# S5 stage of a two-layer encoder: C powers shared between GpSimd and VectorE, start reordered, gate joined to the scan

## The reference

```
u = x @ w_in                                   # 1024 x 1024, 64 groups of 16 channels
lam_bar = exp(lam * step);  b_bar = ((lam_bar - 1) / lam) * b
h_t = lam_bar * h_(t-1) + b_bar @ u_t          # complex, 64 states per group, both directions
y = Re(c @ h) forward + backward + d_skip * u
y = gelu(y);  y = y * sigmoid(y @ w_glu + b_glu);  y @ w_out
```

## Time and profile before

| | |
|---|---|
| median of 3 runs | 3157.04 us |
| the profiled execution's own time | 3158.34 us |
| its span | 3156.5 us |
| start of the 8 scans on VectorE | 96.3, 137.3, 180.3, 218.1, 252.9, 290.6, 324.5, 352.0 us |
| last product of the gate | ends at 500.84 us |

### The profile page before, as it was taken

One profiled execution on the slowest core, in us unless ns is written; L12 is line 12 of the kernel. 1 busy time (PEld: TensorE's weight loads), 2 busy tenths in 40 slices (PEclk: granted clock), 3 DMA queues, 4 the chain that ended last, 5 costly groups with the idle time before them and its releaser, 6 DMA issues. The chain is left out here.

```text
span 3156.5 us, 37141 instructions
## 1 busy us (share of the span) xinstructions
PE 2795.4 (89%) x14372; PEld 2350.9 (74%) x14372; DVE 1446.9 (46%) x2328; ACT 591.5 (19%) x843; POOL 764.4 (24%) x524
## 2 busy tenths in 40 slices
PE   5477588879999999968999999999687999999995
PEld 4366466668888888856888888889476888888884
DVE  5757622463332333262556555556646332233326
ACT  2122233021111111122222222221302111111111
POOL 1899423121221112211011111010402112111122
PEclk7788788989999999988999999996798999999997
DMA  3133212121111111012010100000312111111101
GB/s 115 47 93 96 67 54 107 40 80 40 40 53 53 53 40 40 13 67 53 21 34 20 33 27 27 26 20 1 120 41 77 44 40 53 53 48 45 40 13 67
DMA packets 213106, 157.94 MB, mean 50 GB/s; under 512 B 21792, under 2 KB 196000, under 8 KB 211872
## 3 DMA queue, kind: packets, MB, share of 16 engines
q1 hardware_dynamic: 213024, 156.83, 16.5%
HBM read 139.04 MB, written 17.76 MB: 50 GB/s over the span
## 5 line engine op out<-in xcount | busy, mean ns | idle before, releaser
L463 PE MATMUL ps<-aT_hi,ffn_w_hi 128*128 128x512 f32 x1408 | 555.6, 395 | 18.0 <-PEq L233 18.0
L463 PE MATMUL ps<-aT_hi,ffn_w_lo 128*128 128x512 f32 x1408 | 553.2, 393 | 0.0
L463 PE MATMUL ps<-aT_lo,ffn_w_hi 128*128 128x512 f32 x1408 | 548.2, 389 | 0.0
L546 DVE TENSOR_TENSOR ffn_act_out<-ffn_act_out,ps 128x512 f32<-128x512 f32 x88 | 60.5, 687 | 710.9 <-ACT ffn_act_out L518 710.9
L563 DVE TENSOR_TENSOR h<-h,ps 128x512 f32<-128x512 f32 x352 | 241.8, 687 | 214.6 <-PE ps L477 212.4
L611 POOL CAST ffn_hid_hi<-ffn_act_out 128x512 fp32r<-128x512 f32 x88 | 57.5, 653 | 1114.4 <-PE ps L477 584.4
L463 PEld LDWEIGHTS ps<-aT_hi,ffn_w_hi 128*128 128x128 f32 x1408 | 265.4, 189 | 72.3 <-issue 18.7
L463 PEld LDWEIGHTS ps<-aT_hi,ffn_w_lo 128*128 128x128 f32 x1408 | 265.1, 188 | 61.3
L463 PEld LDWEIGHTS ps<-aT_lo,ffn_w_hi 128*128 128x128 f32 x1408 | 265.2, 188 | 59.6
L477 PE MATMUL ps<-ffn_w_hi,ffn_hid_hi 128*128 128x512 f32 x704 | 275.9, 392 | 6.8 <-POOL ffn_hid_lo L614 6.8
L477 PE MATMUL ps<-ffn_w_hi,ffn_hid_lo 128*128 128x512 f32 x704 | 275.1, 391 | 0.0
(11 more groups left out here) (246 smaller groups left out, 4359.9 us busy)
## 6 DMA issues: line engine op xcount, KB each, us to landing
ffn_w_raw<-in_ffn_w_in_dram SPq DMA_DIRECT2D x88, 512.0 KB, 5.1
ffn_w_raw<-in_ffn_w_out_dram SPq DMA_DIRECT2D x22, 1024.0 KB, 5.0
hg_w_raw<-in_hg_w_in_dram SPq DMA_DIRECT2D x40, 512.0 KB, 4.0
h<-in_x_dram SPq DMA_DIRECT2D x4, 1024.0 KB, 9.1
s_w_raw<-in_s_w_in_dram SPq DMA_DIRECT2D x8, 512.0 KB, 5.1
s_scratch_u<-h SPq DMA_DIRECT2D x16, 256.0 KB, 2.3
s_u_grp<-s_scratch_u SPq DMA_DIRECT2D x64, 64.0 KB, 2.5
s_pw_in<-s_scratch_kern SPq DMA_DIRECT2D x64, 64.0 KB, 2.5
```

The costliest lines, as they stand in the source:

```text
L463: ins = t.matmul(ps[:, 2 * b + a, :], w[q][:, a, kk, :], x[:, kk, rows], start=(kk == 0 and m == 0), stop=(kk == KT - 1 and m == 2))
L546: v.tensor_tensor(act_out[u % 2][:, :], act_out[u % 2][:, :], ps[:, 2 * (u % 2) + 1, :], ALU.mult).then_inc(s_prod, 1)
```

## The change

Four edits, all in the first 501 us.

1. C powers. GpSimd makes only the backward half of cl (from block 1 on). The forward half is made by VectorE ahead of each scan (`make_cl_in_psum`): ScalarE copies the block's C into PSUM bank 2 (`place_c`), the temporary lies in bank 3, and every product has one operand in PSUM. b_all and c_all are stored with the 16 channels of a group contiguous.
2. Start. All 16 transposes and splits of x come before `tables_to_factors`. `scan_factors` squares with four instructions per level in place of six, and the mask of the diagonal moves ahead of the split of x. GpSimd makes bl of block 1 before cl of block 0.
3. The loop's order. TensorE starts with two blocks of `turn_bl` and `start_state` ahead of the loop, and a turn is now `start_state(n)`, `make_kern(n)`, `within_chunks(n-1)`, `across_chunks(n-1)`, `inputs(n+2)`, `turn_bl(n+1)`. y goes straight to its row of h and from there to DRAM.
4. Gate. Weights of the gate are loaded, split and multiplied in the same block: the splits of y rows 0 to 6 and the gate's tiles 0 and 1 up to row 6 stand before the last y. The buffers of `w_in` and bl take the gate's weights.

```diff
+    def make_cl_in_psum(e, n):
+        link = Steps(S["cl_fw"], (n - 1) * CLF)
+        for b in range(2):
+            rows_ = slice(2 * b, 2 * b + 2)
+            c = [bc(c_turned[:, q, rows_, :], 2, [P, 2, L + 1, GRP]) for q in range(2)]
+            out = [cl[n % 2][:, q, rows_] for q in range(2)]
+            t = ps[:, 3, 0:2 * (L + 1) * GRP].rearrange("p (r l c) -> p r l c", r=2, l=L + 1)
+            product_steps(link, e, c, powers(n, 0, rows_), out, t, conj=True)
...
             for n in range(KT):
+                if n == 0:
+                    put_u(2)
+                else:
+                    ungroup_y(n - 1)
                 if 1 <= n < KT - 1:
                     regroup_u(n + 1)
-                if n >= 1:
-                    ungroup_y(n - 1)
                 place_toeplitz(n)
...
+                if n == KT - 2:
+                    load_glu(0)
+            load_glu(1)
             ungroup_y(KT - 1)
...
-            for n in range(KT):
+            for n in range(1, KT):
+                if n >= 2:
+                    start_state(n)
                 make_kern(n)
-                if n >= 1:
-                    across_chunks(n - 1)
+                within_chunks(n - 1)
+                across_chunks(n - 1)
                 if n + 2 < KT:
                     inputs(n + 2, (0, 1))
                 if n + 1 < KT:
                     turn_bl(n + 1)
-                within_chunks(n)
-                if n + 1 < KT:
-                    start_state(n + 1)
...
+            gate_part(0, (0, 1), range(6), (2, 3))
+            within_chunks(KT - 1)
             across_chunks(KT - 1)
+            gate_part(0, (0, 1), (6,), (2, 3))
+            t.wait_ge(S["glu_lo1"], 1)
+            gate_part(1, (0, 1), range(7), (4, 5))
+            gate_part(0, (0, 1), (7,), (2, 3))
+            gate_part(1, (0, 1), (7,), (4, 5))
...
+            def place_c(n):
+                a.wait_ge(S["min_kept"], 4 * (n + 1))
+                a.activation(c_turned, c_all[:, 0, :, n * PR:(n + 1) * PR, :], ACT.Copy).then_inc(S["c_placed"], 1)
...
+                if n == KT - 2:
+                    split_glu(0)
                 if n + 1 < KT:
                     place_b(n + 1)
                     keep_min(n + 1)
+                    place_c(n + 1)
+                gelu(n - 1)
...
+                if n >= KT - 2:
+                    for kk in (range(5) if n == KT - 2 else range(5, 7)):
+                        split_y(kk)
+                if n == KT - 1:
+                    split_glu(1)
                 keep_state(n)
```

More of the change, by code:

```diff
@@ L88, in __init__ @@
         self.nc, self.ctx = nc, ctx
-        self.phase = None
+        self.phase, self.areas, self.deferred = None, [], False
         self.fresh, self.old = [], []
@@ L1229, in _ @@
             split_w(2)
-            for n in range(KT):
+            keep_min(1)
+            place_c(1)
+            keep_u(2)
+            split_w(3)
+            keep_state(0)
+            keep_kern_rows(0)
+            place_b(1)
+            for n in range(1, KT):
                 keep_kern_rows(n)
-                if n >= 1:
-                    keep_y(n - 1)
+                keep_y(n - 1)
                 if n + 2 < KT:
@@ L1245, in _ @@
             gelu(KT - 1)
+            split_y(KT - 1)
+            gates(0)
+            for n in range(1, KT):
+                if n + 1 < KT:
+                    split_glu(n + 1)
+                gates(n)
         @block.vector
@@ L1423, in _ @@
             tables_to_angles()
-            for n in range(2):
+            channel_mask()
+            for n in range(XT):
                 split_x(n)
             tables_to_factors()
-            for n in range(2, XT):
-                split_x(n)
             v.wait_ge(S["b_kept"], 4)
@@ L1434, in _ @@
             v.memset(state[:, :, :, 0], 0.0).then_inc(S["pads"], 1)
+            scan(0)
+            for n in range(1, KT):
+                v.wait_ge(S["c_placed"], n)
+                if n >= 2:
+                    v.wait_ge(S["out_done"], n - 1)
+                make_cl_in_psum(v, n)
+                scan(n)
+            v.wait_ge(S["y_hi"], KT)
+            v.tensor_tensor(k.aT_lo[:, KT - 1, :], row(KT - 1), k.aT_hi[:, KT - 1, :].bitcast(F32), ALU.subtract
+                            ).then_inc(S["y_lo_last"], 1)
             for n in range(KT):
-                scan(n)
+                for half in range(2):
+                    v.wait_ge(S["gated"], 2 * n + half + 1)
+                    o = h[:, n, half * HALF:(half + 1) * HALF]
+                    v.tensor_tensor(o, o, gate[half][:, :], ALU.mult).then_inc(S["mixed"], 1)
         @block.gpsimd
@@ L1585 @@
+                    ins(n + 1)
+                if n + 3 < KT:
+                    split_w(n + 3)
+            split_glu(0)
+            for n in range(7):
+                split_y(n)
+                if n == 5:
+                    split_glu(1)
+            for n in range(2, KT):
+                split_glu(n)
+    k.close_area()
 HG_OUTS = 5
```

324 lines of the change are left out of this document (158 added, 166 removed).

## The result

The changed kernel takes 3101.2 us (median of 4 runs, 3100.69 to 3106.75), the kernel before 3158.1 in the same comparison (4 runs, 3156.69 to 3162.84): a ratio of 0.9821, 95% interval 0.9804 to 0.9838, so 1.6 to 2.0% faster. The forecast was 3105 us, in a range of 3080 to 3128. The profiled execution took 3100.69 (span 3098.9), 57.65 less than the profiled one of before.

What follows compares the result with a forecast made beforehand. The prediction took GpSimd to bound the loop, with VectorE's chain ahead of it. Start -34, period -21 and tail +3 sum to -52 (51.5 before rounding): 3157.0 - 51.5 = 3105 us, range 3080 to 3128.

Steps and rivals of the forecast that it cites:

- Term 1: Start, up to the end of `inputs(3)`: earlier scan factors and block 1 ahead of C, -34 us.
- I1: End of `inputs(3)` on TensorE, where the start ends: forecast at 133 us, against 166.7 before.
- Term 2: Loop period over four turns: from 37.5 to 32.3 us a turn, -21 us.
- the last of the three: Of the chains on GpSimd, VectorE and TensorE in each loop turn, TensorE's ends last, 13.2 us after the turn's start.
- I: End of an `inputs` on TensorE, from which a loop turn's three chains are counted; the next comes 32.3 us later.
- Term 3: Tail to the last gate product: 187 us against 184, +3, its gains mostly spent on two waits for gate weights.
- I5: End of `inputs(7)` on TensorE, where the tail begins: forecast at 262 us, against 316.72 before.
- the three trips: SyncE's y trip (7.4 us), block 7's u (3.8) and block 6's Toeplitz (5.9), ahead of the gate's first load.
- covered waits: Rival in the tail: ScalarE finds the gate's weights already there, scan 7 starts at 41; -71, 3086 us; chance 0.14.
- Held products: Rival in the loop: GpSimd stalls VectorE's C products, 18 us a block; +19, 3176 us; chance 0.04.
- The clock: Rival in the loop: TensorE's clock is low through every turn, period 35; -41, 3116 us; chance 0.20.
- The start: Rival: the start gains nothing net, the first two turns take it back; -7, 3150 us; chance 0.05.

Runs made afterwards that it cites:

- with the load early: Changed kernel with the load of the gate's first weights issued one turn earlier, at the end of turn 5: 3081.3 us.
- the factors alone: Kernel before with one line moved: GpSimd waits for the scan factors before making C of block 0; 3161.2 us.
- the fastest: States first plus four tail edits: both gate loads early, earlier split of y row 5, block 7 products sooner, third tile's low weights on VectorE; 3069.2 us.
- the run from SBUF: Changed kernel with VectorE's C products reading C from SBUF and the temporary in SBUF, so both inputs lie there: 3146.5 us.
- states first: Changed kernel with ScalarE keeping states before placing b_bar, splitting weights and gelu, and GpSimd making C ahead of low weights: 3073.6 us.

## Why the prediction was right

**Term 1** was right in its size (-33.7) and its places: scan 0 at 55.2, scan 1 at 91.2, I1 at 133.0 against 55, 92 and 133. That block 1 must come ahead of C was in the sum only as GpSimd's new order; the runs show that without it 15 us of the term are gone, and that free squarings by themselves are worth nothing in the kernel before.

**Term 2** was right (32.26 us, forecast 32.3), and so was its reason, that TensorE's chain is the last of the three. It is so by little: in the turn shown VectorE's C products end at I + 10.9, GpSimd's at I + 11.9 and `start_state` at I + 12.6 (I is 199.25), and over the four turns GpSimd is ahead of `make_kern` by 0.1 to 2.2 us. Slowing GpSimd's chain by the old layout changed little, and shortening both by another order gave 2.5 us a turn, until VectorE was the bound. In the sum TensorE ends its `start_state` partly at the lower clock; it does, 5.50 against 3.71 us.

**Term 3** named the right wait and mis-sized the tail: 178.7 where the forecast had 187. The load landed at I5 + 39.1, not 42.5: y of block 5 was kept 2 us sooner than counted, the three trips and the load took 1.2 us less, and the forecast's own steps add up to 42.1. Scan 7 started 54.3 behind I5 instead of 58. In turn 7 the states of block 7 were held until 81.3 instead of 91; 6 us of that are in the way from scan 7 to the landing of the second load, for which the forecast gives a figure without steps. From there to the end 97.4 us passed, where the forecast had 96. The removal of the first wait was priced in the prediction (covered waits) at 20 us, 3086; with the load early it is 20, 3081.

**Behind the gate** the forecast had no change and 2.5 us were lost. The code there is the same in all kernels here. From the last gate product to the end of the span their profiled executions take 2655.5 us (the factors alone) to 2658.2 (the changed kernel), and not in the order of what was changed: 2655.7 for the kernel before, but also 2656.0 for the changed kernel in the old layout and 2655.6 for the fastest. So the 2.5 us are a spread between executions and not shown to be an effect of the change. They offset part of the over-counted tail, so the total came out closer (57.65 against 51.5 to 52) than the third term: that much is luck.

**The rivals.** Held products did not happen, and the run from SBUF shows that they would have with both inputs there; their price was counted too high (6.7 us a block, not 12.6). The clock was low in parts of a turn, as forecast, not through all of it. The start was not lost.

## What to carry to other kernels

Where VectorE takes over work of a busy GpSimd, give its instructions one operand in PSUM: with both in SBUF the same split was worth 45 us less. A wait in the middle of an in-order engine's turn is priced by what is queued behind it, not by its length: one of 20 us cost 20 us, or 9 with another order behind it, and taking away one of 5 us gave nothing. And an engine freed early at a start gives less, or nothing, where the engine that the next block waits for begins with work that nobody waits for yet: 13.6 us of it gave nothing in the kernel before, and that order alone cost 14.5 us in the changed one.

## What was not expected of the hardware

A wait of TensorE can cost more than its length, though the same wait doesn't do so every time. In the changed kernel two waits of 2.1 to 2.3 (once 1.2) and 2.6 to 3.9 us, in the middle and at the end of the 16 products of `turn_bl`, stand ahead of each `start_state` of the loop, and it takes 5.1 to 6.4 us in all five turns, where it is 3.71 at full clock; 6.9 us for C were followed by instructions at the lower clock that took 2.6 us longer. With waits of 0.31 and 1.6 to 1.8 us, states first has 3.71 to 3.86 us in three turns and 5.38 in two, and the fastest kernel has a turn like these two:

```profile
195.04 5.38 PE L1120 MATMUL ps<-s_u_grp,s_min 128*64 128x128 f32 x64 [1.83 <-ACT s_state L1272]
```

The hold of VectorE beside GpSimd slows both: VectorE's products of 288 elements go at the pace of GpSimd's instructions, and GpSimd's products of 128 elements went from 0.40 to 0.50 and 0.61 us.
